# Starting addresses of the activations and of Strassen's sums in SBUF

## The chip, the cores and the metric

The program runs on one core of one Trainium2 chip. The metric is the device time in microseconds (us). The kernel before the change has a median of 1122.44 us over three runs (1122.0 to 1122.52).

## The reference

Two transformer blocks follow each other on one sequence of 512 tokens with 1024 features, in float32. Cut to its products:

```python
def first_block(x, ...):
    h = rms_norm(x, norm1_g[l])
    proj = jnp.einsum('bsd,dc->bsc', h, w_in[l])            # 2048 columns
    mix = concat(spatial_gating(u_a, v_a, ...), conformer_conv(val_b, gate_b, ...))
    x = x + jnp.einsum('bsc,cd->bsd', mix, w_out[l])
    h = rms_norm(x, norm2_g[l])
    f = jnp.square(jax.nn.relu(jnp.einsum('bsd,df->bsf', h, w_ff1[l])))   # 4096 columns
    x = x + jnp.einsum('bsf,fd->bsd', f, w_ff2[l])
    return rms_norm(x, final_g)

def second_block(x, ...):
    proj = jnp.einsum('bsd,dc->bsc', rmsnorm(x, g_pre_mix), w_in)
    # attention over the 128 best keys of an indexer, and differential attention
    y = jnp.einsum('bsc,cd->bsd', mix, w_out)
    x = x + rmsnorm(y, g_post_mix)
    u = jax.nn.relu(jnp.einsum('bsd,df->bsf', rmsnorm(x, g_pre_mlp), w_up))
    y = jnp.einsum('bsf,fd->bsd', u * u, w_down)
    return x + rmsnorm(y, g_post_mlp)
```

## The kernel before

**Products in three parts.** Activations lie transposed in SBUF, features on the 128 partitions and tokens along the row. Each float32 operand of a large product is split into a rounded high part and the rest (`xh`, `xl` for the normalised activations, `uh`, `ul` for the squared feed-forward tiles and the mixer's output, `wh`, `wl` for the weights, all of type fp32r), and each product is three matmuls into one PSUM bank: high by high, high by low, low by high. The function `three` issues them on L749, L750 and L751. The second argument of a matmul is loaded as weights, the third moves. Each matmul instruction comes with a weight load of its own (PEld in the profile), and the load for the next matmul begins with the current one.

**Weights.** All weights stream from HBM in chunks of 128 partitions x 1024 values into four slots `raw`; GpSimd (POOL) makes `wh` (L548) and `wl` (L551) of them, in the same order in which PE uses the chunks. Four ways of using a chunk matter here:

- `chunk_transposed` and the interleaved `several`, `first_chunk` and `chunk_highs_first` (L749 to L751, L822 to L832, L942 to L964): weights from `wh` or `wl`, and 512 tokens of `xh` or `xl` move. Four chunks have 384 tokens. With `uh` and `ul` in place of `xh` and `xl` the same function makes the first block's down projection.
- `group_natural` (L781 to L783): 128 tokens of `xh` or `xl` are the weights, and 512 columns of `wh` or `wl` move.
- `rows_group` (L1425 to L1427): `uh` or `ul` are the weights, and `wh` or `wl` move; the second block's down projection.
- `pair` (through `product` and `three`): most of both up projections by Strassen's scheme. Two chunks and 512 tokens give seven products of four k-steps, twelve matmuls with 256 tokens moving, 84 in a pair. They run in the order: `xh` early half, `xh` early half, `t_high[1]`, `t_high[0]`, `t_high[2]`, `xh` late half, `t_high[3]`, each with its low part. `t_high` and `t_low` are sums of activation blocks, made before the first pair by `t_sums` on VectorE (DVE) and `t_round` on ScalarE (ACT). The profile leaves buffer numbers out and calls all four `t_high`.

There are four runs of pairs, `pairs_of(0)` to `pairs_of(3)`, with 4, 8, 4 and 8 pairs. In front of the first and the third run stand eight plain chunks (`feed_first`), behind each run eight or sixteen chunks of the down projection.

**Work beside a pair.** VectorE forms the sums of weight blocks of the next pair (`weight_sums_first` on L2336 and L2338, L2344 and L2345), their low parts (L2353), adds up the products (L2361 to L2394, in the order L2361, L2366, L2371, L2378, L2381, L2388, L2394) and makes the low part of the squared tiles (L2398). L2336 adds two halves of one raw chunk, both in SBUF, into PSUM. ScalarE rounds the sums (L1659), copies the first product and squares. GpSimd splits the chunk that is used as it is: L685 and L688, then L678, L680 and L681, of which L678 waits for PE's second product. PE waits in a pair, among others, for `part_added` and `evacuated` (VectorE's additions, which free banks) and for `sum_ready` (L2353). Behind the second run PE's next chunk waits for L2388 of the last pair, behind the third for L2371, behind the fourth for L2381.

**Addresses.** `sb` hands out SBUF from a running offset `place[0]`, which starts at 16512 (128 modulo 1024). The order is `x`, `xh`, `xl`, `raw` x4, `wh` x4, `wl` x4, `uh`, `ul`, `ident`, `ones`, `center`, `mask`, small tiles, `rb`, `ss`, `sq` x2, small tiles, `tmp` x4, `tmb` x4, small tiles, and then `behind`, a region of 16,384 bytes that other tiles share. The four sums lie in

```python
        t_high = [at(f"t_high{i}", [P, 4, Q], F32R, o) for i, o in
                  enumerate((behind, behind + 8192, tmb_at, tmp_at))]
        t_low = [at(f"t_low{i}", [P, 4, Q], F32R, o + 4096) for i, o in
                 enumerate((behind, behind + 8192, tmb_at, tmp_at))]
```

`x`, `xh`, `xl`, `raw`, `wh`, `wl`, `uh` and `ul` have sizes that are multiples of 1024 bytes, so in the kernel before they all begin 128 bytes above a multiple of 1024. A 128-column weight tile is 512 bytes, so within a chunk the weights' start alternates by 512 modulo 1024.

Of the kernel before, what the change touches and what calls it, by code (L numbers as in the profile page):

```python
# [55 lines left out]
SLOTS = 4  # L56

WARM_MIDDLE = 2


Q = S // 2
# [157 lines left out]
def build(nc, a):  # L219
    ctx = ExitStack()  # L220
    with ctx:
        place = [nc.sbuf_base + (-nc.sbuf_base) % 64]

        def size(shape):
            return 4 * int(np.prod(shape[1:]))

        def at(name, shape, dt, offset):
            return nc.alloc_sbuf_tensor_at(name, shape, dt, offset=offset)

        def sb(name, shape, dt=F32):  # L230
            offset = place[0]
            place[0] += size(shape) + (-size(shape)) % 32
            return at(name, shape, dt, offset)
# [2 lines left out]
            return ctx.enter_context(nc.semaphore(name))  # L236


        x = sb("x", [P, KT, S])
        xh_at = place[0]  # L240
        xh = sb("xh", [P, KT, S], F32R)
        xl_at = place[0]
        xl = sb("xl", [P, KT, S], F32R)
        raw = [sb(f"raw{i}", [P, 1024]) for i in range(SLOTS)]
        wh_at = place[0]
        wh = [sb(f"wh{i}", [P, 1024], F32R) for i in range(SLOTS)]
# [24 lines left out]
        row_weight = sb("row_weight", [P, TB])  # L271
        row_weight_mean = sb("row_weight_mean", [P, TB])
        fgp = sb("fgp", [P, KT])
        tmp_at = place[0]
        tmp = [sb(f"tmp{i}", [P, S]) for i in range(4)]
        tmb_at = place[0]
# [9 lines left out]
        scaled_eps = sb("scaled_eps", [P, DIFF_TILES])  # L286
        diff_gain = sb("diff_gain", [P, 1])
        nlam = sb("nlam", [P, 8])
        behind = place[0]


# [453 lines left out]
        def _(pe):  # L745
# [145 lines left out]
            def norm_spread(i):  # L891

                pe.wait_ge(rn_ready, i + 1)
                r = rn1[:] if i == 6 else rn[:, 4:8] if i in (9, 11) else rn[:, 0:4]
                spread(NB, r).then_inc(bc_done, 1)
# [30 lines left out]
            def keep_warm(turns):  # L926


                for _ in range(turns):
                    mm(bank[0][:], ones[:], mask[:], start=True, stop=True)  # L930
# [465 lines left out]
            norm_spread(12)  # L1396
            keep_warm(WARM_MIDDLE)

# [1584 lines left out]
```

## Time and profile before

| | |
|---|---|
| median of three runs | 1122.44 us |
| span of the profiled execution, first to last instruction | 1120.9 us |
| time of the timed runs around that span (1122.44 - 1120.9) | 1.5 us |
| PE busy | 1110.7 us, 99% |
| DVE, ACT, POOL busy | 704.8, 401.7, 681.6 us |
| TensorE instructions | 6163 matmuls, 6163 weight loads |
| granted TensorE clock | 0.999 on the mean |

The profile is of one execution; its record holds the span, and no time of its own outside it. Durations of matmuls overlap: the next starts before the one before has drained, so a pace is read from the distance between starts.

### The profile page before, as it was taken

The numbers are of one execution on the slowest core, as the hardware profiler recorded it, in microseconds if no ns is written. First come the engines' busy times: TensorE is split into PE (matmuls) and PEld (weight loads), VectorE is DVE, ScalarE is ACT, GpSimd is POOL, SyncE is SP. The second block draws the span as 40 slices with busy tenths as digits, with TensorE's granted clock in tenths as the row PEclk, the third lists the DMA queues.
The fourth block names the chain that finished last, engine by engine and source line by source line (L and its number), as shares of the span: only waits on it lengthen the run. The fifth ranks groups of instructions, "written<-read, shape, count | busy, mean of one in ns | idle before, by whom it ended". The sixth has DMA issues, their size and how long they took to land.

```text
span 1120.9 us, 17261 instructions
## 1 busy us (share of the span) xinstructions
PE 1110.7 (99%) x6163; PEld 940.3 (84%) x6163; DVE 704.8 (63%) x1381; ACT 401.7 (36%) x817; POOL 681.6 (61%) x460
## 2 busy tenths in 40 slices
PE   8999999999999999999999999999999999999997
PEld 6888888998889998888778777677899888999886
DVE  5999778850158853547789777666887113885023
ACT  5156566530015531120202346645665000554012
POOL 7879946586636686667456433135847763558662
PEclk9999999999999999999999999999999999999999
DMA  7321222342213342334343221112224822235412
GB/s 253 131 87 64 75 81 89 112 133 94 94 61 111 113 151 96 107 98 132 113 129 98 84 87 58 38 58 75 76 76 138 183 94 69 86 111 179 160 57 75
DMA packets 52251, 115.54 MB, mean 103 GB/s; under 512 B 21840, under 2 KB 22480, under 8 KB 52176
## 3 DMA queue, kind: packets, MB, share of 16 engines
q1 hardware_dynamic: 31200, 105.40, 28.3%
q10 hardware_dynamic: 20976, 9.15, 3.4%
q8 instruction: 46, 0.75, 0.3%
q14 instruction: 29, 0.24, 0.1%
HBM read 105.09 MB, written 4.19 MB: 97 GB/s over the span
## 4 chain that ended last, share of the span: by engine, by line
PE 96%; ACT 1%; DVE 1%; DMA 0%; issue 0%; SPq 0%; ACTq 0%; DVEq 0%
PE bank L749 21%; PE bank L751 20%; PE bank L750 20%; PE bank L1425 5%; PE bank L1427 5%; PE bank L1426 5%; PE bank L781 2%; PE bank L783 2%; PE bank L782 2%; PE bank L1260 2%; PE bank L822 1%; PE bank L1274 1%; PE bank L832 1%; PE bank L823 1%; PE bank L1214 1%; PE bank L1298 1%
## 5 line engine op out<-in xcount | busy, mean ns | idle before, releaser
L551 POOL TENSOR_TENSOR wl<-raw,wh 128x1024 fp32r<-128x1024 f32 x140 | 337.1, 2408 | 11.7
L548 POOL TENSOR_SCALAR wh<-raw 128x1024 fp32r<-128x1024 f32 x139 | 149.1, 1073 | 258.6 <-PE bank L751 144.0
L749 PE MATMUL bank<-xh,wh 128*128 128x512 f32 (+2 forms) x672 | 234.5, 349 | 0.0
L751 PE MATMUL bank<-xh,wl 128*128 128x512 f32 (+2 forms) x672 | 229.4, 341 | 0.0
L750 PE MATMUL bank<-xl,wh 128*128 128x512 f32 (+2 forms) x672 | 229.1, 341 | 0.0
L749 PEld LDWEIGHTS bank<-xh,wh 128*128 128x128 f32 x672 | 126.8, 189 | 29.1 <-issue 16.6
L1659 ACT ACTIVATE wh<-bank 128x512 fp32r<-128x512 f32 x96 | 52.2, 596 | 253.1 <-DVE bank L2338 109.7
L751 PEld LDWEIGHTS bank<-xh,wl 128*128 128x128 f32 x672 | 126.8, 189 | 14.2
L750 PEld LDWEIGHTS bank<-xl,wh 128*128 128x128 f32 x672 | 126.9, 189 | 12.6 <-issue 0.2
L749 PE MATMUL bank<-uh,wh 128*128 128x512 f32 x288 | 112.8, 392 | 0.0
L751 PE MATMUL bank<-uh,wl 128*128 128x512 f32 x288 | 112.1, 389 | 0.0
L750 PE MATMUL bank<-ul,wh 128*128 128x512 f32 x288 | 112.1, 389 | 0.0
L750 PE MATMUL bank<-t_low,wh 128*128 128x256 f32 x384 | 107.6, 280 | 0.0
L751 PE MATMUL bank<-t_high,wl 128*128 128x256 f32 x384 | 107.3, 280 | 0.0
L749 PE MATMUL bank<-t_high,wh 128*128 128x256 f32 x384 | 107.3, 279 | 0.0
L1426 PE MATMUL bank<-wl,uh 128*128 128x512 f32 x240 | 93.4, 389 | 0.0
L1427 PE MATMUL bank<-wh,ul 128*128 128x512 f32 x240 | 93.4, 389 | 0.0
L1425 PE MATMUL bank<-wh,uh 128*128 128x512 f32 x240 | 93.4, 389 | 0.0
L1986 DVE TENSOR_TENSOR bank<-bank,rb 128x512 f32<-128x512 f32 x16 | 11.2, 699 | 111.4 <-PE bank L751 111.4
L2353 DVE TENSOR_TENSOR wl<-bank,wh 128x512 fp32r<-128x512 f32 x96 | 63.2, 682 | 25.5 <-ACT wh L1659 25.0
L685 POOL TENSOR_SCALAR wh<-raw 128x512 fp32r<-128x512 f32 x24 | 14.9, 620 | 102.7 <-PE bank L751 90.0
L749 PEld LDWEIGHTS bank<-t_high,wh 128*128 128x128 f32 x384 | 72.8, 189 | 0.0
(378 smaller groups left out, 2283.2 us busy)
## 6 DMA issues: line engine op xcount, KB each, us to landing
raw<-wstream SPq DMA_DIRECT2D x188, 512.0 KB, 3.5
x<-xT SPq DMA_DIRECT2D x8, 256.0 KB, 4.8
x4rows<-x_rows ACTq DMA_DIRECT2D x4, 512.0 KB, 9.1
out<-x4rows SPq DMA_DIRECT2D x8, 256.0 KB, 2.1
qd<-ropey ACTq DMA_DIRECT2D x16, 64.0 KB, 2.2
kd<-ropey ACTq DMA_DIRECT2D x16, 64.0 KB, 2.1
qa<-ropey SPq DMA_DIRECT2D x16, 64.0 KB, 2.0
ka<-ropey SPq DMA_DIRECT2D x16, 64.0 KB, 2.0
```

The source lines that it names most:

```text
L548: nc.gpsimd.tensor_scalar(wh[c][:], raw[c][:], 1.0, 1.0, ALU.mult, ALU.mult).then_inc(high_ready, 1)
L551: nc.gpsimd.tensor_tensor(wl[c][:], raw[c][:], wh[c][:].bitcast(F32), ALU.subtract).then_inc(split_ready, 1)
L749: mm(out, wh_, mh, start=start, stop=False)
L750: mm(out, wh_, ml, start=False, stop=False)
L751: return mm(out, wl_, mh, start=False, stop=stop)
L781: mm(out, xh[:, k, ts], wh[s][:, ws], start=k == 0, stop=False)
L782: mm(out, xh[:, k, ts], wl[s][:, ws], start=False, stop=False)
L1425: mm(out, uh[:, f, ts], wh[s][:, ws], start=f == 0, stop=False)
L1426: mm(out, uh[:, f, ts], wl[s][:, ws], start=False, stop=False)
L1427: last = mm(out, ul[:, f, ts], wh[s][:, ws], start=False, stop=f == 15)
L1659: A(wh[slot_of(p, role)][:, 512 * part:512 * part + 512], bank[7 - made % 2][:], ACT.Copy).then_inc(sum_rounded, 1)
L2353: V.tensor_tensor(wl[slot][:, at], bank[7 - made % 2][:], wh[slot][:, at].bitcast(F32), ALU.subtract).then_inc(sum_ready, 1)
```

## The change

Two constants and a helper `start_at` move the running offset up to a given rest modulo 1024. Four calls place `xh` and `xl` at 832 modulo 1024, `raw` and all that follows it at 128 again, and `tmp` and `behind` at 832. Relative to the weights, `xh` and `xl` come from 0 to 704 modulo 1024; `tmp` and `tmb` were at 704 and stay there; `behind` comes from 864 to 704. `x`, `uh`, `ul` and the constants keep their place modulo 1024. No instruction is added, taken away or moved in order. The last tile ends 1,888 bytes higher, still inside SBUF.

```diff
+WEIGHTS_AT = 128
+MOVED_AT = 832
+
...
+        def start_at(rest):
+
+            place[0] += (rest - place[0]) % 1024
+
         x = sb("x", [P, KT, S])
+        start_at(MOVED_AT)
         xh_at = place[0]
         xh = sb("xh", [P, KT, S], F32R)
         xl_at = place[0]
         xl = sb("xl", [P, KT, S], F32R)
+        start_at(WEIGHTS_AT)
         raw = [sb(f"raw{i}", [P, 1024]) for i in range(SLOTS)]
...
         fgp = sb("fgp", [P, KT])
+        start_at(MOVED_AT)
         tmp_at = place[0]
         tmp = [sb(f"tmp{i}", [P, S]) for i in range(4)]
...
         nlam = sb("nlam", [P, 8])
+        start_at(MOVED_AT)
         behind = place[0]
```

## Rows read from the trace of the kernel before

**Rows 1.** Page: busy time of each engine; the chain by engine.

```profile
PE 1110.7 (99%) x6163; PEld 940.3 (84%) x6163; DVE 704.8 (63%) x1381; ACT 401.7 (36%) x817; POOL 681.6 (61%) x460
...
PE 96%; ACT 1%; DVE 1%; DMA 0%; issue 0%; SPq 0%; ACTq 0%; DVEq 0%
```

**Rows 2.** Waits of PE: us in total, times, longest.

```profile
PE bank L969 <- DVE tmp L2040: 1.5, 1, 1.5
```

**Rows 3.** Timeline of PE in a pair of the second run: start, duration, instruction.

```profile
355.10 0.28 PE L749 MATMUL bank<-xh,wh 128*128 128x256 f32 x1
...
356.52 0.28 PE L749 MATMUL bank<-xh,wh 128*128 128x256 f32 x1
...
357.96 0.28 PE L749 MATMUL bank<-t_high,wh 128*128 128x256 f32 x1
...
360.85 0.28 PE L749 MATMUL bank<-t_high,wh 128*128 128x256 f32 x1
...
361.31 0.28 PE L750 MATMUL bank<-t_low,wh 128*128 128x256 f32 x1
...
362.22 0.28 PE L749 MATMUL bank<-xh,wh 128*128 128x256 f32 x1
...
363.64 0.29 PE L749 MATMUL bank<-t_high,wh 128*128 128x256 f32 x1
...
365.02 0.28 PE L749 MATMUL bank<-xh,wh 128*128 128x256 f32 x1
```

**Rows 4.** Timeline of PE in a plain chunk of 512 columns.

```profile
187.05 0.39 PE L751 MATMUL bank<-xh,wl 128*128 128x512 f32 x1
...
188.64 0.39 PE L749 MATMUL bank<-xh,wh 128*128 128x512 f32 x1
```

**Rows 5.** Windows: length, busy us (instructions) per engine, granted clock, DMA share, GB/s.

```profile
0.00:20.00 20.00, 17.16 (x57) 10.67 (x58) 13.03 (x17) 12.88 (x20) 13.61 (x26) 1.00 0.79 284
...
776.00:821.30 45.30, 45.17 (x204) 36.64 (x203) 39.66 (x75) 32.78 (x70) 27.53 (x18) 1.00 0.18 59
...
861.00:948.00 87.00, 87.00 (x386) 72.08 (x385) 18.52 (x27) 5.61 (x10) 52.06 (x32) 1.00 0.47 122
```

**Rows 6.** Chain in order of time, matmuls with one moving column: start, us.

```profile
497.85 0.87 PE bank L847 x8
```

**Rows 7.** Groups of PE by line and form: count, busy us, mean ns.

```profile
L749 PE MATMUL bank<-xh,wh 128*128 128x512 f32 x352 | 142.4, 404 | 0.0
...
L781 PE MATMUL bank<-wh,xh 128*128 128x512 f32 x96 | 38.0, 395 | 0.0
...
L749 PE MATMUL bank<-xh,wh 128*128 128x384 f32 x32 | 11.0, 343 | 0.0
```

**Rows 8.** Timeline of VectorE in pairs of the second and third run.

```profile
339.93 1.52 DVE L2336 TENSOR_TENSOR bank<-raw 128x512 f32<-128x512 f32 x1
...
360.45 0.84 DVE L2336 TENSOR_TENSOR bank<-raw 128x512 f32<-128x512 f32 x1
...
367.67 0.41 DVE L2394 TENSOR_TENSOR pair_buffer<-bank,pair_buffer 128x256 f32<-128x256 f32 x1
...
403.49 0.42 DVE L2388 TENSOR_TENSOR ss<-bank,ss 128x256 f32<-128x256 f32 x1 [0.67 <-PE bank L751]
...
838.61 0.69 DVE L2336 TENSOR_TENSOR bank<-raw 128x512 f32<-128x512 f32 x1
...
848.38 0.69 DVE L2336 TENSOR_TENSOR bank<-raw 128x512 f32<-128x512 f32 x1
...
859.53 0.41 DVE L2371 TENSOR_TENSOR ss<-bank,second_sum 128x256 f32<-128x256 f32 x1
```

**Rows 9.** Timeline of GpSimd in the pair of rows 3.

```profile
359.43 1.30 POOL L680 TENSOR_TENSOR wl<-raw,wh 128x512 fp32r<-128x512 f32 x1
360.68 1.74 POOL L681 TENSOR_TENSOR wl<-raw,wh 128x512 fp32r<-128x512 f32 x1
```

## The prediction

> **What bounds the kernel.** I read the page first: the matmul engine is busy for 99% of the span and the chain that ended last is 96% PE; VectorE and GpSimd are at 63% and 61% [rows 1]. The waits of PE confirm it: 1.5 us for the longest, at the start [rows 2]. So the time is, to a few us, the number of matmuls times their pace. "Mean ns of one" doesn't give that pace, since matmuls overlap; the distance between starts does, and I took it from the timeline. At the granted clock of 1.00 (2.4 GHz) a matmul of 256 columns needs 106.7 ns to stream, one of 512 needs 213.3 ns.
>
> One Strassen pair is the right place to look, because it contains three placements of the moving operand against the weights, with the same shape, the same three lines and the same weights' tiles. Modulo 1024, `xh` and `xl` begin where `wh` and `wl` begin (0). From `ident` to `tmp` the sizes add up to 12,992 bytes, so `tmp` and `tmb`, which hold the third and fourth sums (`t_high[2]`, `t_high[3]`), lie 704 off; 17,568 bytes later `behind`, which holds the first two sums, lies 864 off. The seven products of twelve matmuls come in the order x, x, sum 1, sum 0, sum 2, x, sum 3. The starts [rows 3] give 1.42 and 1.44 us for the first two, 2.89 for the next two together, and 1.37, 1.42 and 1.38 us for the last three. Per matmul that is 120 ns at 0 (a little less right behind a product at 704), 120 at 864, and 114 to 115 at 704. The two at 704 still pay for the change of placement in their first matmuls; the last eight of the fifth product run from 361.31 to 362.22, 113.3 ns each. So the offset shows in the time of before: 6.7 ns per matmul between 0 and 704.
>
> At 512 columns only offset 0 exists. With `xh` moving, seven matmuls take 1.59 us, 227 ns each [rows 4]. With `uh` as weights the 384 of one group of rows take the 87 us from 861 to 948 (the row counts one more at each edge), 227 ns as well [rows 5]. That is 13.5 ns over the streaming time, and 120 is 13.3 over it at 256 columns: the excess doesn't grow with the width. I read it as a cost per matmul, paid while the next weights are read: that read begins with each matmul and is over in about 110 ns, the pace of matmuls with one moving column (0.87 us for 8) [rows 6].
>
> **The change part by part.** It adds no instruction. It moves tiles by up to 1,888 bytes, so the cost is paces only.
>
> Pairs. All sums and all of `xh`, `xl` come to 704. Modulo 1024 the starts for successive k alternate by 512, which the sums at 704 do too, so I take 113.3 ns for all 84: 9.52 us in place of 9.92 [rows 3], 0.40 us for each of 24 pairs, 9.6 us.
>
> Matmuls of 512 columns with `xh` or `xl` moving: 352 on each of L749 to L751 and 210 on the lines of the interleaved chunks (L822 to L832 and L942 to L964), 1,266 in all; 96 more have 384 columns [rows 7]. Their price at 704 is in no row. Below: nothing, if only the narrow ones care. Above: 13.3 ns, since they can't beat the streaming time. I take 6.7 ns, the row of 256 columns, because the first 256 columns of a wide matmul meet the same weight read as a narrow one: 8.5 + 0.6 = 9.1 us.
>
> Natural-order chunks, 288 matmuls on L781 to L783 (96 on each) [rows 7]: here `xh` is the weights and `wh` moves, so the offset is -704, that is 320 or 832. The nearest row is 864, whose 24 average 120 ns [rows 3]; modulo 512 it is 352, near 320. So I take zero; bounds 6.7 ns either way, 1.9 us.
>
> Products with `uh`, `ul` (down projections, first part of the output projection) keep offset 0: zero. DMA, GpSimd's splitting (61% busy) and ACT have room.
>
> In full that is 9.6 + 9.1 = 18.7 us. What of it is not kept:
>
> The first 20 us wait for loads; the 53 wide matmuls among the 57 there [rows 5] give nothing: 0.4 us.
>
> VectorE in the pairs. Its loop free of others is 9.77 us: the starts of L2336 in two pairs of the third run, 838.61 and 848.38 [rows 8]. Against 9.92 that was enough, against 9.52 it isn't. In the steady pairs it is held by GpSimd: L2336 has both inputs in SBUF and takes 0.84 us in place of 0.69 when it arrives at 360.45, and 1.52 when it arrives at 339.93; at 360.45 it ends 0.56 us after GpSimd's L680 does, and L681, beside it, takes 1.74 [rows 8, 9]. L680 follows PE's second product. With pairs of 9.52 us L680 ends 5.4 us after the pair's start (now 5.6), L2336 of the next pair comes at 6.0 + 9.08 - 9.52 = 5.56 (now 5.35), and finds L681 started: held until about 6.7, VectorE then loses 1.1 us once and 0.25 us per pair. PE's tightest wait in a pair is for L2394 of the pair before, in front of its fifth product: it ends at 368.07 [rows 8] against 360.85 + 9.92 = 370.77 [rows 3], 2.7 us of slack, 2.1 with pairs of 9.5, so PE holds its pace through about eight pairs. But at the end of an 8-pair run VectorE is some 2.4 us late. The next chunk waits for L2388, which now starts at 403.49, as soon as the sixth product is done, one product before PE needs it [rows 8]. Late by 2.4 us, L2361 starts 7.5 us after the pair's start, and the additions behind it, back to back, end at 10.6 against 9.5: PE waits 1.0 us, and about 0.7 in the last run, where the wait is for the addition before: 1.7 us in two runs. The 4-pair run at 198 us has room.
>
> The stage from 776 to 861 us. VectorE is busy 39.7 of the first 45.3 us and ACT 32.8 [rows 5]; their turns, not PE, set when the sums for the third run are ready. PE would gain 1.25 us in the chunks (186 wide among the 204) and 1.6 in the four pairs. It may come early at the following group of rows by only as much as L2371, which ends at 859.94, lies ahead of PE's 861.0 [rows 5, 8]: 1.1 us. Lost: 1.75 us.
>
> 18.7 - 0.4 - 1.7 - 1.8 = 14.8 us. The profiled execution has a span of 1120.9 us, so its span should come to 1106.1; the timed runs have a median of 1122.44, 1.5 us more, which lies around the span and stays: **1107.6 us**.
>
> **What speaks against it.** The rows say that placement costs PE 6.7 ns per matmul. The Trainium skill says otherwise, on the page "SBUF — State Buffer", section "Who interferes with whom": PE has two independent read ports, one for the moving operand and one for the weights, and PE and ACT never wait for anyone. By that rule no offset could matter and the time would stay at 1122.4; the trace disagrees, 113.3 against 120 ns [rows 3]. Its outcome is that of rival (c).
>
> **Rivals.**
> (a) Only narrow matmuls gain. At 256 columns the weight read fills the matmul, at 512 it leaves 100 ns to make up a delay. For it: no wide row at 704. Against: the excess at offset 0 is the same 13.3 to 13.5 ns at both widths. It gives 9.6 - 1.7 - 0.5 (of the four pairs' 1.6 all but 1.1) = 7.4 us: 1115.
> (b) The wide ones gain nearly all 13 ns, because what is left at 113.3 is the weight read's own 110 ns [rows 6], which a wide matmul hides. About 1,130 of the wide ones can use it (not those before 20 us and in the stage that VectorE sets), 6.6 ns more each, 7.5 us: 1100.
> (c) No change. The fast products are fast by something else that the third and fourth sums share, their region or their VectorE neighbours, and the move carries nothing over: 1122.4. Against: `xh` in one region and `uh` in another, both at 0, have one pace [rows 4, 5], and it is the low bits that they share.
> (d) Slower. At 512 columns the moving read passes 2,048 bytes, twice the modulus, and at 704 meets the weights later rather than not at all; the phase that suits 256 columns costs at 512. The pairs bring 7.4 us as in (a), so it decides from 5.8 ns on for each of 1,266. Against: no row shows a placement that costs more on the mean than 0 does. At 9 ns, 236 for 227, the time is 1122.4 - 7.4 + 11.4 = 1126.
>
> **How the numbers follow.** Chances: the forecast with its VectorE waits 0.52, (a) 0.20, (b) 0.16, (c) 0.06, (d) 0.06. The range reaches from (b) with half of the natural chunks' bound, 1099, to (a) and 1 us more of waits for VectorE, 1116; outside lie (c), (d) and the edges of (a) and (b). A measurement here tells about 0.2% (2.2 us) from no change: faster 0.88, within it 0.06, slower 0.06.
>
> **What would show it.** In the timeline of PE all products of a pair at 113 to 114 ns and pairs 9.5 us apart; chunks with `xh` moving at 220 ns (227 speaks for (a), 216 for (b), 232 or more for (d)); chunks of `uh` still at 227; the natural chunks near 227. In VectorE's timeline L2336 coming later from pair to pair in the runs of eight, one of them taking 1.5 us or more; PE waiting for VectorE behind the runs of eight and in the third run. I am wrong in sign if the wide chunks slow down, and in size mostly by the wide chunks' pace.

## The result

The changed kernel takes 1128.91 us (median of four runs, 1127.27 to 1129.32); the kernel before took 1122.38 us in the four runs beside it. The ratio is 1.0054, 95% interval 1.0042 to 1.0066: slower by 0.5%. The forecast was 1107.6 us, from 1099 to 1116, so the sign is wrong. Lines of the changed kernel stand 11 higher: L749 is L760, L2336 is L2347, L2388 is L2399.

Page of the changed kernel, busy time:

```profile
span 1127.1 us, 17261 instructions
...
PE 1117.0 (99%) x6163; PEld 940.5 (83%) x6163; DVE 704.9 (63%) x1381; ACT 401.8 (36%) x817; POOL 682.5 (61%) x460
```

PE has gained 6.3 us of busy time with the same 6163 matmuls [rows 1], and its longest wait is still the one of the start:

```profile
PE bank L980 <- DVE tmp L2051: 1.5, 1, 1.5
```

So the loss is again one of pace, the time from the start of one matmul to the start of the next. First a pair of the second run, timeline of PE, first matmul of each of the seven products and of the next pair (start, duration, instruction); it answers to [rows 3]:

```profile
357.60 0.28 PE L760 MATMUL bank<-xh,wh 128*128 128x256 f32 x1
...
359.01 0.28 PE L760 MATMUL bank<-xh,wh 128*128 128x256 f32 x1
...
360.43 0.28 PE L760 MATMUL bank<-t_high,wh 128*128 128x256 f32 x1
...
361.84 0.28 PE L760 MATMUL bank<-t_high,wh 128*128 128x256 f32 x1
...
363.25 0.28 PE L760 MATMUL bank<-t_high,wh 128*128 128x256 f32 x1
...
364.67 0.28 PE L760 MATMUL bank<-xh,wh 128*128 128x256 f32 x1
...
366.08 0.28 PE L760 MATMUL bank<-t_high,wh 128*128 128x256 f32 x1
...
367.49 0.28 PE L760 MATMUL bank<-xh,wh 128*128 128x256 f32 x1
```

All seven products now have one pace, as expected of one placement, but it is 1.41 us for twelve, 117.8 ns each, and not 113.3. The pair takes 9.89 us (367.49 - 357.60) in place of 9.92. The fifth and the seventh product, whose addresses were not changed, have become slower: 1.37 and 1.38 us before, 1.41 now.

Then a plain chunk with `xh` moving, answering to [rows 4]:

```profile
189.61 0.40 PE L760 MATMUL bank<-xh,wh 128*128 128x512 f32 x1
...
192.88 0.40 PE L762 MATMUL bank<-xh,wl 128*128 128x512 f32 x1
```

There are 14 steps between these two: 3.27 us / 14 = 233.6 ns, against 227 before. The group with `uh` as weights, whose placement is the same, has kept its pace: its 384 matmuls take 87.06 us from start to start in either kernel, 226.7 ns each. A window over most of it (the first of the 381 instructions runs in from before, the last are narrow ones of the next run of pairs):

```profile
868.95:954.75 85.80, 85.80 (x381) 71.13 (x380) 17.73 (x26) 3.29 (x6) 50.49 (x31) 1.00 0.50 123
```

Summed over the trace, from start to start: the wide matmuls with `xh` or `xl` moving cost 5.8 us more (the 1,056 on L760 to L762 5.2 ns each, 5.5 us; the interleaved ones about 5 ns each, 1.0 us; the rest, which wait for loads, 0.6 us less), the natural-order chunks 0.6 us more, the 24 pairs 0.5 us less, and the 96 matmuls of 384 columns 0.1 us more. Unrounded that is 5.9 of the 6.2 us between the spans.

### The profile page after: what moved, and what is told of

It is laid out like the page before. It is cut to its first block, busy times and chain, and to the rows that moved or that the text cites. A ratio compares the mean times of both kernels' runs of the same rounds, so it can differ in the third digit from the quotient of the medians.

```text
span 1127.1 us, 17261 instructions
## 1 busy us (share of the span) xinstructions
PE 1117.0 (99%) x6163; PEld 940.5 (83%) x6163; DVE 704.9 (63%) x1381; ACT 401.8 (36%) x817; POOL 682.5 (61%) x460
## 4 chain that ended last, share of the span: by engine, by line
PE 96%; ACT 1%; DVE 1%; DMA 0%; issue 0%; SPq 0%; DVEq 0%; ACTq 0%
PE bank L760 21%; PE bank L761 21%; PE bank L762 21%; PE bank L1437 5%; PE bank L1436 5%; PE bank L1438 5%; PE bank L794 2%; PE bank L793 2%; PE bank L792 2%; PE bank L1271 2%; PE bank L833 1%; PE bank L1285 1%; PE bank L834 1%; PE bank L843 1%; PE bank L1225 1%; PE bank L1309 1%
## 5 line engine op out<-in xcount | busy, mean ns | idle before, releaser
L760 PE MATMUL bank<-xh,wh 128*128 128x512 f32 (+2 forms) x672 | 236.0, 351 | 0.0
L762 PE MATMUL bank<-xh,wl 128*128 128x512 f32 (+2 forms) x672 | 230.8, 343 | 0.0
L760 PEld LDWEIGHTS bank<-xh,wh 128*128 128x128 f32 x672 | 126.2, 188 | 30.7 <-issue 16.4
L762 PEld LDWEIGHTS bank<-xh,wl 128*128 128x128 f32 x672 | 127.0, 189 | 16.0
L760 PE MATMUL bank<-uh,wh 128*128 128x512 f32 x288 | 112.7, 391 | 0.0
L762 PE MATMUL bank<-uh,wl 128*128 128x512 f32 x288 | 112.1, 389 | 0.0
L760 PE MATMUL bank<-t_high,wh 128*128 128x256 f32 x384 | 107.9, 281 | 0.0
L762 PE MATMUL bank<-t_high,wl 128*128 128x256 f32 x384 | 107.9, 281 | 0.0
L696 POOL TENSOR_SCALAR wh<-raw 128x512 fp32r<-128x512 f32 x24 | 14.9, 619 | 103.8 <-PE bank L762 91.1
L762 PEld LDWEIGHTS bank<-t_high,wl 128*128 128x128 f32 x384 | 73.2, 191 | 0.0
```

Source lines behind the costliest of these rows:

```text
L760: mm(out, wh_, mh, start=start, stop=False)
L762: return mm(out, wl_, mh, start=False, stop=stop)
```

## The experiments

"The distance" is that of the moving operand from the weights. Theory A: the distance sets the pace of every matmul, for each width by a table of its own. Rivals stand in the expectations; the one that mattered came out of the sweep (theory C): the distance and the pace or phase in which PE arrives set it together. A pair of the second run is read in each kernel, where nothing else is said, and pairs are given as starts from pair to pair.

**1 to 3. The parts of the change, each from the kernel before.** `e1_shift` moves weights and all behind them by 1024 bytes, so that no distance changes modulo 1024. `e2_sums` moves only the first two sums. `e3_x` moves only `xh` and `xl`.

```diff
 e1_shift            xl = sb("xl", [P, KT, S], F32R)
+                    place[0] += 1024
 e2_sums             nlam = sb("nlam", [P, 8])
+                    start_at(832)
                     behind = place[0]
 e3_x                x = sb("x", [P, KT, S])
+                    start_at(832)
                     xh_at = place[0]
...
+                    start_at(128)
                     raw = [sb(f"raw{i}", [P, 1024]) for i in range(SLOTS)]
```

> The kernel before, with raw, wh, wl and everything behind them 1024 bytes further up, xh and xl where they were: no distance modulo 1024 changes, every absolute address behind xl does, as in the changed kernel. If only the distance modulo 1024 counts (theory A), this is the kernel before: 1122.4 us within 0.2%, wide matmuls on xh at 227 ns, the fifth and seventh product of a pair at 113 to 115 ns. If the absolute address or a larger modulus counts (theory B), those two products come at 118 ns as in the changed kernel, and a pair takes 9.92 + 2 x 12 x 3.5 ns = 10.0 us, the total 1124.

Measured: 1122.3 us, ratio 1.0 (0.999 to 1.001), with the same products fast and slow. Moving the weights by 1024 bytes changes nothing, so the loss doesn't hang on their absolute address.

> Only the last padding: behind, with the first two sums, from 864 to 704; xh and xl stay at 0. Theory A: products three and four go from 120 to 113.3 ns, the seven products add up to 9.76 us, the total falls by 24 x 0.16 = 3.9 us to 1118.5 and wide matmuls stay at 227 ns. Theory C (the pace is a property of a settled stream and depends on what ran before, not of one placement): the sums' products may settle at another pace, such as the 118 ns of the changed kernel, and the gain is half of it or nothing.

Measured: 1118.75 us, ratio 0.9969 (0.9957 to 0.998). Timeline of its pair:

```profile
353.69 0.28 PE L753 MATMUL bank<-xh,wh 128*128 128x256 f32 x1
...
356.55 0.29 PE L753 MATMUL bank<-t_high,wh 128*128 128x256 f32 x1
357.93 0.28 PE L753 MATMUL bank<-t_high,wh 128*128 128x256 f32 x1
359.29 0.28 PE L753 MATMUL bank<-t_high,wh 128*128 128x256 f32 x1
360.65 0.28 PE L753 MATMUL bank<-xh,wh 128*128 128x256 f32 x1
...
363.45 0.28 PE L753 MATMUL bank<-xh,wh 128*128 128x256 f32 x1
```

The three sums in a row take 1.38, 1.36 and 1.36 us: the first pays for the change of placement, the others run at 113.3 ns. The pair takes 9.76 us, 0.15 less than before, 24 times 0.15 = 3.6 us, of the 3.8 that the time shows. This half of the change is a gain.

> Only xh and xl at 704; behind stays at 864. All theories: wide matmuls on xh at 233 ns as in the changed kernel, 1266 x 6.7 = 8.4 us more. Pairs by theory A: products one, two and six at 113 us per thousand (113 ns), three and four at 120, so 9.7 us a pair and 5 us less, together 1126. Theory C: some other pace around 118, pairs near 9.9 us and 1130 in total.

(In it, 113 us per thousand means 113 ns for each matmul.) Measured: 1128.56 us, ratio 1.0055 (1.0038 to 1.0072). Wide matmuls take 233 ns. So moving `xh` and `xl` carries the whole loss. In the two runs of eight pairs a pair takes 9.95 us: the narrow products with `xh` didn't come to 113 ns but to 117 to 118, and the third and fourth sum, unmoved at 704, went from 114 to 118 with them. In the two runs of four, with the same placements, a pair takes 9.69 us, and the products with `xh` run at 113.3 ns. Timeline of a pair of the first run, then of one of the second, its first matmul and that of the next pair:

```profile
210.59 0.28 PE L754 MATMUL bank<-xh,wh 128*128 128x256 f32 x1
...
220.28 0.28 PE L754 MATMUL bank<-xh,wh 128*128 128x256 f32 x1
```

```profile
337.13 0.28 PE L754 MATMUL bank<-xh,wh 128*128 128x256 f32 x1
...
347.07 0.28 PE L754 MATMUL bank<-xh,wh 128*128 128x256 f32 x1
```

All four runs begin alike, with two products at 1.41 us; behind the sums at 864 the runs of four go on at 113.3 ns and the runs of eight at 117.8. The runs of four stand behind wide matmuls with `xh` (at 704), the runs of eight behind wide ones with `uh` (at 0). Theory A's table cannot give two paces for one placement in one kernel, and since the pace of the first two products is the same in both, the pace with which PE arrives isn't the whole of its history either.

**4. Streams of matmuls alone.** A kernel of its own: it loads weights, runs `three`'s order of matmuls in segments of one distance, and stores; it computes nothing of the reference, and no other engine works beside it.

```diff
+ SEGMENTS = [(0, 512, 0, 32)] + [(off, 512, 0, 16) for off in STEPS] + ...  # STEPS: 0, 64, ... 960
+ mm(out_, wh_, mh, start=i == 0, stop=False)
+ mm(out_, wh_, ml, start=False, stop=False)
+ last = mm(out_, wl_, mh, start=False, stop=i == turns - 1)
```

> The disputed cost by itself: no work of the reference, only streams of the same three matmuls (wh by mh, wh by ml, wl by mh) with nothing else running. The distance of the moving operand from the weights goes through 0, 64, ..., 960 bytes modulo 1024, 48 matmuls each, first with 512 and then with 256 columns; then 704 and 0 again with weights and moving operand both 1024 bytes further; then groups of twelve narrow matmuls in the order of a pair, once with all sums at 704 and once with the first two at 864 less 32. Theory A: 227 ns at 0 and 233 at 704 for 512 columns, 120 at 0 and 113 at 704 for 256, the same 1024 bytes further. Theory B: the streams 1024 bytes further differ. Theory C: 704 at 256 columns settles at one pace or the other by what ran before it. If none of it shows (216 ns at every distance), other engines' traffic makes the difference, not PE's two reads.

Windows of five segments of 48 matmuls (start:end, length, PE busy with its instructions, of which one or two run in from before, granted clock, DMA share, GB/s): 512 columns at 0 and at 704, 256 columns at 0 and at 704, and 256 columns at 704 again, but this time entered from wide matmuls at 0.

```profile
57.81:68.68 10.87, 10.87 (x49) 1.00 0.00 0
179.37:190.56 11.19, 11.19 (x49) 1.00 0.00 0
240.58:246.33 5.75, 5.75 (x50) 1.00 0.00 0
302.82:308.29 5.47, 5.47 (x50) 1.00 0.01 3
352.96:358.60 5.64, 5.64 (x49) 1.00 0.00 0
```

Divided by 48: 226.5 and 233.1 ns wide; 119.8 and 114.0 ns narrow (113.3 once settled); and 117.5 ns for the same narrow distance after wide matmuls. The paces repeat every 256 bytes, not every 1024 (wide: 226.7 at 0, 256, 512 and 768; 228.9 at 64, 232.1 at 128, 233.3 at 192). 704 is 192 modulo 256, and 864 is 96. The last window is the first sign of history: one distance and one width have two paces. Its weights and moving operand both lie 1024 bytes further up, which the next run leaves out. The groups of twelve say the same: in the order of a pair with all sums at 704 they take 1.44, 1.44, 1.38, 1.36, 1.36, 1.42 and 1.38 us, nearly the pair of `e2_sums`, but 704 entered from narrow matmuls at 832 (64 modulo 256, 117.8 ns) stays at 117.5 ns. So it isn't only wide matmuls that lead to the slow pace.

**5. Finer steps, and the way in.** The same kernel in steps of 16 bytes; each narrow segment is entered once from narrow and once from wide matmuls.

```diff
+ [(16 * i, 512, 0, 16) for i in range(16)]
+ [s for i in range(16) for s in ((0, 256, 0, 8), (16 * i, 256, 0, 12))]
+ [s for i in range(16) for s in ((0, 512, 0, 6), (16 * i, 256, 0, 12))]
+ [s for i in (8, 12, 15) for s in ((192, 512, 0, 6), (16 * i, 256, 0, 12))]
```

> Streams alone again, the distance now 0, 16, ..., 240 bytes, since the sweep repeated every 256 bytes (226.7, 228.9, 232.1, 233.3 ns at 0, 64, 128, 192 for 512 columns; 120.0, 117.8, 118.8, 113.3 for 256). Narrow streams are entered twice, from a narrow stream at 0 and from a wide one at 0, and three of them from a wide one at 192. Theory C, that the phase from before decides at some distances: the narrow stream at 192 comes at 113.3 ns when it follows a narrow one at 0 and at 117.8 when it follows a wide one; at 0 both come to 120. Theory A: one pace per distance, 113.3 at 192, whatever came before. For 512 columns both expect the lowest pace at or near 0; a distance with under 226 ns would be a better place for xh and xl.

Windows of 36 narrow matmuls at distance 192, entered from narrow at 0, from wide at 0 and from wide at 192 (columns: length, busy time of PE, PEld, DVE, POOL with instructions, granted clock, DMA share, GB/s):

```profile
324.17:328.26 4.09, 4.09 (x38) 4.09 (x37) 0.00 (x0) 0.00 (x0) 1.00 0.02 4
454.12:458.35 4.23, 4.23 (x37) 4.22 (x36) 0.00 (x0) 0.00 (x0) 1.00 0.02 4
496.09:500.32 4.23, 4.23 (x37) 4.22 (x36) 0.00 (x0) 0.00 (x0) 1.00 0.02 4
```

4.09 us against 4.23: 113.3 ns once settled against 117.7, and the slow pace doesn't mend itself in 36 matmuls. That is the changed kernel: each run of pairs is entered from wide matmuls, and with one distance in the whole pair it never leaves the slow phase. Wide matmuls were between 226.7 (0 and 240) and 234.5 ns (160 and 208). Other distances depend on the way in too (144: 118.7 ns from narrow, 116.7 from wide). At 112 narrow ones settled at 113.3 from either side, after nine to eleven uneven ones.

**6. The two theories inside the kernel.** The changed kernel with `behind` back at distance 0, that is with two products placed worse.

```diff
-        start_at(MOVED_AT)
+        start_at(WEIGHTS_AT)
         behind = place[0]
```

> The changed kernel with the first two sums (behind) at 0 in place of 704: two of seven products of a pair move with a distance of 0. Theory C: these two run at 120 ns and put the stream back into the phase from which 704 settles at 113.3, so the other five cost about 1.37 us each and a pair 9.75 instead of 9.89 us; total 1128.9 - 3.4 = 1125.5 us, although two products are placed worse. Theory A with 118 ns as the pace of 704 in this kernel: 5 x 1.41 + 2 x 1.44 = 9.93 us a pair, total 1129.8.

Measured: 1124.67 us, ratio to the kernel before 1.0021 (1.0012 to 1.0031), so 4.2 us less than the changed kernel. Timeline of its pair:

```profile
356.98 0.28 PE L760 MATMUL bank<-xh,wh 128*128 128x256 f32 x1
358.34 0.28 PE L760 MATMUL bank<-xh,wh 128*128 128x256 f32 x1
359.70 0.28 PE L760 MATMUL bank<-t_high,wh 128*128 128x256 f32 x1
361.12 0.28 PE L760 MATMUL bank<-t_high,wh 128*128 128x256 f32 x1
362.56 0.29 PE L760 MATMUL bank<-t_high,wh 128*128 128x256 f32 x1
...
366.66 0.28 PE L760 MATMUL bank<-xh,wh 128*128 128x256 f32 x1
```

The two worse products take 1.42 and 1.44 us, and all others, whose placement is that of the changed kernel, have come from 1.41 to between 1.36 and 1.38. The pair takes 9.68 us. History is shown in the kernel, not only in a stream.

The faster pair also shows what the prediction said of VectorE. Its timeline, L2347 (L2336 before) in four pairs:

```profile
342.21 1.45 DVE L2347 TENSOR_TENSOR bank<-raw 128x512 f32<-128x512 f32 x1
...
352.75 1.85 DVE L2347 TENSOR_TENSOR bank<-raw 128x512 f32<-128x512 f32 x1
...
363.69 0.69 DVE L2347 TENSOR_TENSOR bank<-raw 128x512 f32<-128x512 f32 x1
...
373.47 0.69 DVE L2347 TENSOR_TENSOR bank<-raw 128x512 f32<-128x512 f32 x1
```

It is held at 352.75 for 1.85 us, after that it is free at 0.69, and its starts are 9.78 us apart where pairs are 9.68. PE's waits:

```profile
PE bank L760 <- DVE ss L2399: 0.3, 1, 0.3
```

**7. The modulus.** The changed kernel with `xh`, `xl` at distance 256 and the sums at 704.

```diff
         x = sb("x", [P, KT, S])
-        start_at(MOVED_AT)
+        start_at(WEIGHTS_AT + 256)
```

> The changed kernel with xh and xl 256 bytes off the weights in place of 704; all sums stay at 704. If the period is 256 bytes, 256 is as good as 0: wide matmuls at 227 ns, products on xh at 120, on the sums at 113, and the time of the kernel with only the sums moved, 1118.7 us. If the period is 1024 as the change assumes, 256 is a place like any other and the wide matmuls come at another pace, probably between 227 and 233 ns, 1119 to 1127 us.

Measured: 1118.8 us, ratio 0.9969 (0.9956 to 0.9981), product by product the trace of `e2_sums`, where `xh` is at 0. So 256 is as good as 0, which with the streams makes the period 256.

**8. What the distance acts on.** The stream kernel again: offsets in steps of 4 bytes around 0, and weight tiles and moving operands that lie in turns at two distances, so that a moving operand lies at one distance from its own weights and at another from the weights that are loaded beside it.

```diff
+ (236, 240, 244, 248, 252, 4, 8, 12) for 512 and for 256 columns
+ TURNS = ((0, 128, 0, 128, 512), (0, 128, 128, 0, 512), ...)   # weights A, B; moving A, B; columns
```

> Streams alone. First part: distances 236 to 256 and 0 to 12 bytes in steps of 4, with 512 and with 256 columns, since 240 had 226.7 ns wide (as 0) and 117.2 narrow (0 has 120): a distance with which both it and its negative stay at 226.7 and narrow matmuls come under 120 would suit xh and xl. Second part: two weight tiles A and B in turn, 512 columns. In the second pattern every matmul is 0 off its own weights, but 128 off the weights that are loaded while it streams; in the third it is 128 off its own and 0 off the next; the sixth and seventh do the same with 192. If what counts is the read of the next weights during the stream (theory N), the second and sixth come near 232 and 233 ns and the third and seventh at 227; if the matmul's own weights count (theory O), the other way round. The first, fourth, fifth and eighth are uniform: 227, 232, 227, 233 by both.

Own distance 0 with the next weights at 128: 228.3 ns; own 128 with the next at 0: 230.0; both at 128: 231.7. For 192 both mixed cases take 231.7 and the uniform one 233.3; there the other of the two distances is 64 in every second matmul. Neither distance alone accounts for it. 4 bytes already count (237.5 ns at 4, 240 at 244), and at 240 wide matmuls took 233.3 ns entered from 0, but 226.7 in run 5, where they were entered from 224: wide matmuls have two phases too. And narrow matmuls at 192 took 117.8 ns when they followed narrow ones at 8, which run at 120 ns sharp just as those at 0 do, from which 192 came to 113.3 (run 5). So it isn't the pace on arrival that decides, but something that the pace doesn't tell. What happens in the memory is left open.

**9 and 10. Placing the weights of the pairs instead.** The kernel before, with all sums at 128 modulo 256 like `xh`, and the weight tiles that the pairs use 144 or 64 bytes up in slots of 4352 bytes. So wide products keep distance 0, and the whole pair has distance 112 (-144) or 192 (-64). The small buffers in the same slots move along, a few small tiles are packed together to make room, and `start_at` counts modulo 256 in runs 9 to 12.

```diff
+SLOT_BYTES = 4352
-        wh = [sb(f"wh{i}", [P, 1024], F32R) for i in range(SLOTS)]
+        wh = [at(f"wh{i}", [P, 1024], F32R, wh_at + i * SLOT_BYTES) for i in range(SLOTS)]
+        pair_high = [at(f"pair_high{i}", [P, 1028], F32R, wh_at + i * SLOT_BYTES + PAIR_SHIFT)[:, PAIR_FIRST:PAIR_FIRST + 1024] for i in range(SLOTS)]
...
-                high_a, low_a = wh[slot_of(p, 0)], wl[slot_of(p, 0)]
+                high_a, low_a = pair_high[slot_of(p, 0)], pair_low[slot_of(p, 0)]
```

> xh, xl and all wide work stay at 0. The weights of the pairs alone lie 144 bytes further up in their slots, and the four sums at 0, so that all seven products of a pair have the distance 112, which came to 113.3 ns in the streams whatever ran before. Theory C and A: pairs of 9.52 us on PE, wide matmuls still 227 ns. If VectorE's loop of 9.77 us then counts as I predicted, one L2336 per run of eight takes 1.5 us or more, VectorE falls back by 0.25 us per pair, PE waits 1 to 2 us at the ends of the runs of eight and in the third run: 1122.4 - 9.6 + 2.2 = 1115.0 us. If VectorE has room, 1112.8 us.

> The same kernel with the pairs' weights 64 bytes up: all seven products at the distance 192 (704 of the change, modulo 256), entered from wide matmuls at 0. Theory C, the phase from before: 192 entered from a wide stream at 0 stays at 117.8 ns, as in the streams, nothing in the run resets it, pairs of 9.89 us as in the changed kernel, total 1122.4 - 0.6 = 1121.8 us. Theory A: 113.3 ns, the time of the run at 112.

Measured: 1126.09 us (ratio 1.0033, 1.0021 to 1.0045) and 1121.95 us (0.9995, 0.9986 to 1.0004). Timeline of a pair in each, its first matmul and that of the next pair:

```profile
355.85 0.28 PE L757 MATMUL bank<-xh,pair_high 128*128 128x256 f32 x1
...
365.93 0.28 PE L757 MATMUL bank<-xh,pair_high 128*128 128x256 f32 x1
```

```profile
355.35 0.28 PE L757 MATMUL bank<-xh,pair_high 128*128 128x256 f32 x1
...
365.24 0.28 PE L757 MATMUL bank<-xh,pair_high 128*128 128x256 f32 x1
```

At 192 the pair takes 9.89 us, 117.8 ns each, the locked phase of the changed kernel, as theory C said; its time follows (24 times 0.02 = 0.5 us less than before). At 112 it failed: 10.08 us, matmuls alternating between 119 and 121 ns, where the stream had settled at 113.3. That is 24 times 0.16 = 3.9 us more, against a measured loss of 3.6. Either 112 has a slow phase too, which no way in that the streams tried led to, or it matters that here the weights were moved (to 16 modulo 64) and in the streams the moving operand; no run separates the two. At 192 moving either one gives the same 117.8 ns.

**11 and 12. Leaving the slow phase on purpose.** From `e10_pair192`, with one or two of the seven products at distance 0 (`t_low` moves like `t_high`).

```diff
 e11_two_at_0
-        start_at(128)
+        start_at(192)
         behind = place[0]
 e12_one_at_0
-                  enumerate((behind, behind + 8192, tmb_at, tmp_at))]
+                  enumerate((behind, behind + 8192 + 64, tmb_at, tmp_at))]
```

> The kernel before with the weights of the pairs 64 bytes up, so that the activations and the third and fourth sums lie 192 bytes (modulo 256) off them, and the region of the first two sums 64 bytes up too, so that these lie at 0. The wide products keep distance 0. The same without the second shift gave 117.7 ns for every narrow matmul and 1121.95 us. Theory C, the pace depends on the distance and on the pace that the engine came with: the two products at 0 break the slow phase, the other five run at 113.3 ns, the pair takes 9.70 us as in the run with mixed places, 24 times 0.22 us less than before, less 0.3 us of waits for VectorE: 1117.5 us (1116.8 to 1118.3). Rival, the address alone sets the pace, 117.7 at 192 and 120 at 0: the pair takes 9.94 us and the time is 1123.0.

> The same, but only the sum of the third product (the second of the four) lies at 0, the other three and the activations at 192. Theory C: the first two products of a run of pairs take 117.7 ns, the third about 120, and from the fourth on all but every seventh 113.3: pairs of 9.60 us, 0.31 us less than before, 7.5 us in 24 pairs; VectorE, whose own loop takes 9.77 us, falls 0.17 us behind per pair and 1.1 us where GpSimd holds it, so PE waits for it at the end of the two runs of eight and in the third run: 1.5 to 2.5 us. 1116.9 us (1116.0 to 1118.0), no better than the run beside it by more than 1 us although a pair is 0.10 us shorter. Rival, the address alone: 9.92 us and 1122.5.

Measured: 1118.05 us (ratio 0.996, 0.9946 to 0.9974) and 1117.47 us (0.9953, 0.9939 to 0.9966; before beside them 1122.19), both as theory C said and 5 us from the rival's 1123.0 and 1122.5. The second is the fastest kernel found; its interval overlaps the first's. Timeline of a pair in `e12_one_at_0`:

```profile
353.07 0.28 PE L757 MATMUL bank<-xh,pair_high 128*128 128x256 f32 x1
354.43 0.28 PE L757 MATMUL bank<-xh,pair_high 128*128 128x256 f32 x1
355.79 0.28 PE L757 MATMUL bank<-t_high,pair_high 128*128 128x256 f32 x1
357.21 0.29 PE L757 MATMUL bank<-t_high,pair_high 128*128 128x256 f32 x1
...
362.67 0.28 PE L757 MATMUL bank<-xh,pair_high 128*128 128x256 f32 x1
```

One product of 1.42 us at the worse distance buys 1.36 to 1.38 for the six others: 9.60 us for the pair, against 9.89 with all seven at 192. Of the 24 times 0.31 = 7.5 us (9.91 before, 9.60 now) only about 5 reach the end. The first pair of each run still begins in the slow phase and takes 9.72 us, 0.5 us in four runs; most of the rest is PE waiting for VectorE. L2344 (L2336 before) and what GpSimd does beside it, first VectorE's timeline, then GpSimd's:

```profile
348.98 1.77 DVE L2344 TENSOR_TENSOR bank<-raw 128x512 f32<-128x512 f32 x1
...
359.85 0.69 DVE L2344 TENSOR_TENSOR bank<-raw 128x512 f32<-128x512 f32 x1
369.62 0.69 DVE L2344 TENSOR_TENSOR bank<-raw 128x512 f32<-128x512 f32 x1
```

```profile
348.90 1.30 POOL L689 TENSOR_TENSOR pair_low<-raw,pair_high 128x512 fp32r<-128x512 f32 x1
...
358.49 1.31 POOL L689 TENSOR_TENSOR pair_low<-raw,pair_high 128x512 fp32r<-128x512 f32 x1
```

At 348.98 it comes 0.08 us behind GpSimd's start and is held until that is done (350.20); a pair later it comes 0.05 us after GpSimd's end (359.80) and is free, but it is now late, and stays at 9.77 us per pair. At the end of the run PE pays:

```profile
PE bank L757 <- DVE ss L2396: 0.8, 1, 0.8
```

That costs 0.9 us from start to start. At the end of the fourth run PE's next chunk comes 0.4 us late. The waits don't name VectorE there, but the chunk starts 0.10 us after L2389 (L2381 before), for which it waits, has ended (1022.07):

```profile
1021.66 0.41 DVE L2389 TENSOR_TENSOR pair_buffer<-bank,ss 128x256 f32<-128x256 f32 x1
```

```profile
1022.17 0.47 PE L1433 MATMUL bank<-wh,uh 128*128 128x512 f32 x1 [0.27 <-issue]
```

In the third run the pairs take 9.74, 9.79, 9.60 and 9.83 us: there PE gains 0.7 us in four pairs, not 1.2. In the second of them a gap of 0.19 us behind the first matmul is followed by a product at 1.41 us, so PE is back in the slow phase until the product at 0.

## Why the prediction was wrong

**What held.** PE's pace sets the time to within 0.3 us: in runs 2, 9 and 10, 24 times the difference of the pairs is the difference of the times, and in the changed kernel the sums of starts give 5.9 of 6.2 us. The offset matters, and 1024 bytes of absolute address don't. Products with `uh` kept 227 ns. The natural-order chunks, taken at zero with 1.9 us for bound, cost 0.6: with a modulus of 256 their -704 is 64, and 64 costs 2.2 ns in the stream (228.9 for 226.7), 0.6 us for 288. By the rule of the Trainium skill cited in the prediction ("SBUF — State Buffer", "Who interferes with whom": two independent read ports) no run could have differed, and the measurement decides against it for this kind of matmul, with 113.3 to about 123 ns at 256 columns and 226.7 to 240 at 512 in streams with no other engine at work.

**The step that failed** is the wide term: "I take 6.7 ns, the row of 256 columns, because the first 256 columns of a wide matmul meet the same weight read as a narrow one". Its size was right and its sign wrong. 704 costs a wide matmul 6.7 ns in a stream, and 5.2 ns on the mean in the chunks: +5.8 us in place of -8.5. The 96 matmuls of 384 columns, put at -0.6 by the same price, changed by +0.1. No row of before had a wide product off distance 0, so a price was carried from one shape to another by a mechanism that no row showed. The bounds were wrong for the same reason: "Below: nothing" left out a loss, although the rows gave no reason for that, and rival (d), a loss at 512 columns by the phase that suits 256, got 0.06. (Its reason, that 2,048 bytes are twice the modulus, was tested by nothing.)

**The second failure** is the pair term, "so I take 113.3 ns for all 84": 0.02 us per pair instead of 0.40, 0.5 us instead of 9.6. The rows were read rightly, 113.3 ns at 704, but as a property of the placement. In [rows 3] both fast products stand behind one at another distance, and the text took the uneven first matmuls as the price of the change of placement, when the change was what led to the fast phase. With the same distance in all products and wide ones in front, PE stays at 117.7 ns (the changed kernel, run 10, and the stream of run 5); runs 6, 11 and 12 get the 113.3 ns back by placing one or two products worse. The modulus was 256 and not 1024, which changed only the natural-order term.

Together: -18.7 us predicted in full, +5.9 measured in the starts; 14.9 of the 24.6 us between them are the wide term with the 384 columns, 9.1 the pairs, 0.6 the natural chunks. The prediction's 110 ns for a weight read, on which (a) and (b) lean, was worked out from one-column matmuls, and no run tested it.

**Rivals.** (a) and (b) needed 113.3 ns in the pairs and fell with it. (c) was to be decided by the fast products being fast "by something else"; half of it was true, but that was their neighbours on PE and not their region. (d) named the right sign, and gave 1126 by two errors that cancel in part: 9 ns for each wide matmul, and 7.4 us of gain in the pairs.

**VectorE.** In the changed kernel L2347 takes 0.80 to 0.82 us in the steady pairs, and nothing is late, since pairs stayed at 9.89. The terms "not kept" were tested where pairs are faster. L2336 was held once by GpSimd for 1.1 to 1.2 us more than its free 0.69, then free, with 9.77 us per pair: seen in runs 6 and 12. PE's wait at the end of the second run was put at 1.0 us for pairs of 9.52; it is 0.8 for 9.60. In the last run, put at 0.7, PE comes 0.4 us late in run 12. The third run's own gain is cut to 0.7 of 1.2 us, in kind as expected.

## What to carry to other kernels

A pace that differs between two groups of matmuls may belong to what ran before them: before moving data to the place of the fast group, look for a fast one that follows its own kind, and one that doesn't change. Where operand placement matters, change one tile at a time and read each width by itself, since 192 bytes off the weights has the lowest pace found for 256 columns, in its fast phase, and one of the higher ones for 512. Here `e2_sums`, a line that moves two sums, brings 0.3%, and `e12_one_at_0` 0.5%.

## What the hardware showed

- The start-to-start pace of fp32r matmuls with a weight load each depends on the distance of the moving operand from the weights modulo 256 bytes: 226.7 ns at 0, 233.3 at 192 and 240 at 244 for 512 columns; 120 at 0, and 113.3 or 117.7 at 192 for 256 columns.
- The paces seen with every matmul alike are 113.33, 120, 226.67 and 233.33 ns (272, 288, 544 and 560 cycles at a granted clock of 1.00, 2.4 GHz), multiples of 16, and 230.0 ns (552 cycles) where the distance changed from matmul to matmul in run 8. The others, 117.7 and 240 among them, are means over uneven ones that repeat.
- The same distance and width have two stable paces, depending on what came before (192: 113.3 and 117.7 narrow; 240: 226.7 and 233.3 wide). The slow one at 192 followed wide matmuls, and narrow ones at 64 or 8; it isn't the pace before that decides, since 0 and 8 both run at 120. Products at 0 led back to the fast one in every run that had them (6, 11, 12); products at 864 did in two runs of pairs of `e3_x` and not in the other two. At 112 a stream settles at 113.3 ns and the kernel at 120. What in the access to memory makes these phases, and why 112 is slow in the kernel, stays open.
